# Two stacked transformer blocks: attention heads of the second block issued between its projections, and four difference heads per transpose

## What is computed

```python
proj = h @ w_in                      # 1024 x 2212
# c_q 384, c_kv 256, k_rope 32, dq dk dv 256 each, fq fk fv 256 each, ff 4
o_mla = mla_attention(rms_norm(c_q) @ w_uq, rms_norm(c_kv) @ w_ukv, k_rope)   # 8 heads, q and k 96 wide
o_diff = diff_attention(dq, dk, dv)  # 4 heads; each two softmaxes over q, k 32 wide
o_fox = forgetting_attention(fq, fk, fv, cumsum(log_sigmoid(ff + bias)))      # 4 heads, 64 wide
h = layer_norm(ALPHA * h + concat(o_mla, o_diff, o_fox) @ w_out)
h = layer_norm(ALPHA * h + grouped_moe(h))   # 16 experts, 2 chosen per token
```

## Time and profile before

| | us |
|---|---|
| median of 3 runs | 1852.04 (1848.75 to 1855.86) |
| profiled execution | 1850.06, its span 1848.3 |
| TensorE busy | 1588.5 (86%), granted clock 0.932 of full |
| VectorE busy | 938.5 (51%) |
| ScalarE busy | 622.3 (34%) |
| DMA | 231 GB/s over the span |
| layer 0: input projection's end to output projection's end | 990.7 to 1107.2 |
| layer 1: the same | 1442.0 to 1561.5 |

### The profile page before, as it was taken

How to read it: one execution, slowest core, us unless ns; L and a number is a source line. 1 busy time by engine, 2 the same in 40 slices (tenths; PEclk the granted TensorE clock), 3 DMA queues, 4 the chain that set the end, 5 groups by cost and what they waited for, 6 DMA issues and landing times.

```text
span 1848.3 us, 18868 instructions
## 1 busy us (share of the span) xinstructions
PE 1588.5 (86%) x7511; PEld 1095.8 (59%) x7511; DVE 938.5 (51%) x1346; ACT 622.3 (34%) x879; POOL 31.5 (2%) x62
## 2 busy tenths in 40 slices
PE   2889987999699987999977875999879696799985
PEld 2677766788587765888856763333327675433331
DVE  5896666855588665654375745111026575411002
ACT  1335534344334453444333631111124371211111
POOL 2000000000000000000030000000000000000000
PEclk9999998999899997999989886999999897799998
DMA  9676355856487433765464034999975404499994
GB/s 336 227 277 204 114 168 196 312 181 224 148 298 273 140 133 114 246 198 194 162 170 158 13 116 192 410 409 409 409 307 177 137 1 185 192 410 409 409 409 192
DMA packets 149964, 427.65 MB, mean 231 GB/s; under 512 B 8105, under 2 KB 16545, under 8 KB 149873
## 3 DMA queue, kind: packets, MB, share of 16 engines
q1 hardware_dynamic: 146192, 417.43, 61.7%
q0 software_dynamic: 3456, 8.87, 1.7%
q10 hardware_dynamic: 224, 0.07, 0.0%
HBM read 425.30 MB, written 1.05 MB: 231 GB/s over the span
## 4 chain that ended last, share of the span: by engine, by line
PE 45%; DVE 7%; SPq 6%; DMA 2%; ACT 1%; issue 1%; DVEq 0%
PE gp L1978 12%; PE gp L2150 9%; PE gp L2310 8%; SPq L702 6%; PE gp L2329 4%; PE mp L2350 2%; DMA raw_more<-in_exp_w_up 2%; PE gp L2295 2%; PE mp L2169 1%; PE mp L2208 1%; PE mp L2219 1%; PE mp L2218 1%; PE mp L2227 1%; DVE stats L1573 1%; DVE wlo L1153 0%
## 5 line engine op out<-in xcount | busy, mean ns | idle before, releaser
L1226 DVE TENSOR_TENSOR wlo<-raw,whi 128x2048 fp32r<-128x2048 f32 (+1 forms) x132 | 289.5, 2193 | 223.0 <-ACT whi L803 221.9
L803 ACT ACTIVATE whi<-raw 128x2048 fp32r<-128x2048 f32 (+1 forms) x132 | 242.2, 1836 | 365.3 <-PE gp L1978 200.5
L1978 PE MATMUL gp<-whi,xt_hi 128*128 128x512 f32 (+1 forms) x800 | 317.4, 397 | 32.2 <-DVE xt_lo L1275 14.1
L1978 PE MATMUL gp<-wlo,xt_hi 128*128 128x512 f32 (+1 forms) x800 | 311.3, 389 | 0.0
L1978 PE MATMUL gp<-whi,xt_lo 128*128 128x512 f32 (+1 forms) x800 | 311.1, 389 | 0.0
L1978 PEld LDWEIGHTS gp<-whi,xt_hi 128*128 128x128 f32 x800 | 154.6, 193 | 72.6 <-DVE wlo L1226 17.7
L1978 PEld LDWEIGHTS gp<-whi,xt_lo 128*128 128x128 f32 x800 | 154.3, 193 | 31.1
L1978 PEld LDWEIGHTS gp<-wlo,xt_hi 128*128 128x128 f32 x800 | 154.7, 193 | 29.1 <-issue 0.2
L1846 DVE TENSOR_SCALAR pr<-slots,key,dg 128x128 f32<-128x128 f32 x64 | 19.3, 344 | 260.1 <-PE gp L2340 260.1
L1153 DVE TENSOR_TENSOR wlo<-raw,whi 128x2048 fp32r<-128x2048 f32 (+3 forms) x36 | 68.3, 1906 | 42.4 <-ACT whi L949 41.8
L1136 DVE SCALAR_TENSOR_TENSOR acc<-raw,cact,acc 128x1024 f32<-128x1024 f32 x69 | 88.4, 1282 | 1.5
(11 more groups left out here) (384 smaller groups left out, 2352.1 us busy)
## 6 DMA issues: line engine op xcount, KB each, us to landing
raw<-in_w_in SPq DMA_DIRECT2D x60, 1024.0 KB, 6.0
raw<-in_w_ada SPq DMA_DIRECT2D x42, 1024.0 KB, 5.4
raw_deep<-in_exp_w_down SPq DMA_DIRECT2D x36, 1024.0 KB, 16.9
raw_deep<-in_exp_w_gate SPq DMA_DIRECT2D x30, 1024.0 KB, 14.4
raw_deep<-in_exp_w_up SPq DMA_DIRECT2D x30, 1024.0 KB, 16.8
raw<-in_w_gate SPq DMA_DIRECT2D x20, 1024.0 KB, 5.2
raw<-in_w_up SPq DMA_DIRECT2D x20, 1024.0 KB, 5.2
raw<-in_w_down SPq DMA_DIRECT2D x20, 1024.0 KB, 5.0
```

Source lines behind the costliest of these rows:

```text
L803: act.activation(slot(whi, s % SPLIT, units, cols), slot(raw, g % RAW, units, cols), ACT.Copy).then_inc(hi_done.sem, 1)
L1226: dve.tensor_tensor(slot(wlo, s % SPLIT, units, cols), slot(raw, g % RAW, units, cols), slot(whi, s % SPLIT, units, cols).bitcast(F32), AL ...
L1978: mm = pe.matmul(gp[:, q % 2, t, 0:wide], a[:, chunk, ts], w[:, unit, c0:c0 + wide], start=first and n == 0 and m == 0, stop=last and n == ...
```

## The change

- The column groups of the input projection are taken in reverse: the 164-column group (last part of fv, and the gates) first, c_q and c_kv last.
- Jobs are reordered: fox (4), diff (8), MLA (8). Each engine's part of step i becomes a function `attend(i)`. Steps 0 to 3 follow input products 6 to 9, steps 4 to 7 stand around the latents' norm and transposes, steps 8 to 11 follow the four up-projection products, and steps 12 to 23 run alone.
- Gates' logarithms, cumulative sum, fox operands, rotations of the diff heads and of the shared key are moved under the input products; the latents' norm moves behind the last of them. The latents are transposed into banks of `gp`, since `mp` is in use.
- Four halves of diff heads lie side by side in 128 columns, so q and k are transposed for four jobs at once (2 turns in place of 8); scores then read rows 0, 32, 64 or 96 of `qkt`.
- Token half 0 of keys and values is copied by ScalarE.
- The difference's first three stages are issued behind steps 16 to 18 on VectorE. Of the turned result, columns 0 to 511 (MLA heads) are transposed before the output projection, the others after its first product; the difference's last stage stands between.

The core of the diff (leading blanks cut):

```diff
+IN2_COLS = [(COLS * j, min(COLS, IN2 - COLS * j)) for j in reversed(range(IN2_JOBS))]
...
+JOBS = [MH + 2 * DH + i for i in range(FH)] + [MH + i for i in range(2 * DH)] + list(range(MH))
+FIRST_DIFF, FIRST_MLA = FH, FH + 2 * DH
+TOGETHER = P // DW
+TURNED = FH + 2 * DH // TOGETHER + MH
...
+def turn_of(i):
+    if i < FIRST_DIFF:
+        return i
+    return FIRST_DIFF + (i - FIRST_DIFF) // TOGETHER if i < FIRST_MLA else i - FIRST_MLA + TURNED - MH
+IN_STEPS = 4
+NORM_STEPS = IN_STEPS + 3
...
+def turned_here(i):
+    return i < AJ and (i == 0 or turn_of(i) != turn_of(i - 1))
+def turn_width(i):
+    return P if FIRST_DIFF <= i < FIRST_MLA else job_width(JOBS[i])
 def job_operands(j):
...
+latent_banks = (gp[:, 1, 0, :], gp[:, 1, 1, :], gp[:, 0, 0, :])
...
+    def attend(i):
+        if turned_here(i):
+            act.wait_ge(*t2_done.at2(l, turn_of(i) + 1))
+            w = turn_width(i)
+            act.activation(qkt[0:w, turn_of(i) % 2, :], mp[0:w, 0, :], ACT.Copy).then_inc(t2_taken.sem, 1)
...
+    high_x(X2_IN)
+    for s in range(S2_UQ):
+        split(s + 2)
+        if s % 2:
+            c, wide = IN2_COLS[s // 2]
...
+        if s >= S2_UQ - IN_STEPS:
+            attend(s - (S2_UQ - IN_STEPS))
+    act.wait_ge(*pair_free[0].at2(l, 6))
+    act.wait_ge(*pair_free[1].at2(l, 4))
+    for t in range(NT):
+        act.activation(rt1[:, 0:CQ], pr[:, t, 0:CQ], ACT.Square, accum_out=lsum4[:, t:t + 1]).then_inc(mla_sq.sem, 1)
+        act.activation(rt2[:, 0:CKV], pr[:, t, CQ:CQ + CKV], ACT.Square, accum_out=lsum4[:, 2 + t:3 + t]).then_inc(mla_sq.sem, 1)
+        act.wait_ge(*mla_sq.at2(l, 2 * t + 2))
+    attend(IN_STEPS)
+    act.wait_ge(*rv2_ready.at2(l, 1))
+    act.activation(rs[:, 0:4], rv[:, 0:4], ACT.Sqrt).then_inc(rs2_ready.sem, 1)
+    for i in range(IN_STEPS + 1, NORM_STEPS):
+        attend(i)
+    for b in range(3):
+        n = 2 if b < 2 else 1
+        high(latent_banks[b], X2_MLA + b, mt_hi[:, 2 * b:2 * b + n, :], n)
+    attend(NORM_STEPS)
+    for s in range(S2_UQ, S2_OUT):
+        split(s + 2)
+        q = J2_UQ + s - S2_UQ
+        h = 4 * ((s - S2_UQ) % 2)
+        if s < S2_UKV:
+            take(q, qm[:, 0, h:h + 4, :].rearrange("p h d -> p (h d)"))
+        else:
+            kv = gp[:, q % 2, 0, :].rearrange("p (h d) -> p h d", h=4)
+            act.wait_ge(*w_used.at2(l, job2_end(q) + 1))
+            act.activation(km[:, 0, h:h + 4, 0:MN], kv[:, :, 0:MN], ACT.Copy).then_inc(kv_taken.sem, 1)
+            act.activation(vm[:, 0, h:h + 4, :], kv[:, :, MN:MN + HD], ACT.Copy).then_inc(kv_taken.sem, 1)
+            act.wait_ge(*kv_taken.at2(l, 2 * (s - S2_UKV) + 2))
+            act.sem_inc(pair_free[q % 2].sem, 1)
+        attend(NORM_STEPS + 1 + s - S2_UQ)
...
+    def forget_gates(stage):
+        if stage == 0:
+            dve.wait_ge(*pair_free[0].at2(l, 2))
+            lk(dve.tensor_tensor(fz[:, :, :], pr[:, :, C_FF:C_FF + FH], fbc[:, :].unsqueeze(1).broadcast_to((P, NT, FH)), ALU.add))
+            lk(dve.tensor_scalar(fe[:, :, :], fz[:, :, :], -1.0, None, ALU.mult))
+            dve.tensor_tensor(fe[:, :, :], fz[:, :, :], fe[:, :, :], ALU.min).then_inc(fz_ready.sem, 1)
+        if stage == 1:
+            dve.wait_ge(*lam_exp.at2(l, 1))
+            lk(dve.tensor_tensor(nlam[:, :], lame[:, 1:2], lame[:, 0:1], ALU.subtract))
+            lk(dve.tensor_tensor(nlam[:, :], nlam[:, :], lami[:, :], ALU.subtract))
+            dve.wait_ge(*fl_ready.at2(l, 1))
+            lk(dve.tensor_scalar(fz[:, :, :], fz[:, :, :], 0.0, None, ALU.min))
+            dve.tensor_tensor(fz[:, :, :], fz[:, :, :], fl[:, :, :], ALU.subtract).then_inc(logf_ready.sem, 1)
+        if stage == 2:
+            dve.wait_ge(*pair_free[1].at2(l, 2))
+            dve.wait_ge(*pair_free[0].at2(l, 4))
+            up = HD ** 0.5
+            for dst, c in ((fq, C_FQ), (fk, C_FK)):
+                lk(dve.tensor_copy(dst[:, :, :, 0:HD], pr[:, :, c:c + FH * HD].rearrange("p t (h d) -> p t h d", d=HD)))
+            lk(dve.memset(fq[:, :, :, HD + 1:HD + 2], 1.0))
+            lk(dve.memset(fk[:, :, :, HD:HD + 1], 1.0))
+            dve.wait_ge(*cum_done.at2(l, 1))
+            cum = mp[:, 3, 0:NT * FH].rearrange("p (t h) -> p t h", t=NT)
+            lk(dve.tensor_scalar(fq[:, :, :, HD:HD + 1].rearrange("p t h a -> p t (h a)"), cum, up, None, ALU.mult))
+            dve.tensor_scalar(fk[:, :, :, HD + 1:HD + 2].rearrange("p t h a -> p t (h a)"), cum, -up, None, ALU.mult).then_inc(fox_ready.sem, 1)
+    def rotate_diff():
+        dve.wait_ge(*pair_free[1].at2(l, 4))
+        for c in (C_DQ, C_DK):
+            rotate(pr[:, :, c:c + 2 * DH * DW].rearrange("p t (h d) -> p t h d", d=DW)[:, :, :, 0:DROT], 2, 2 * DH, DROT)
+        dve.sem_inc(diff_ready.sem, 1)
+    def shared_key():
+        kr = pr[:, :, C_KR:C_KR + KR].unsqueeze(2)
+        rotate(kr, 1, 1, KR)
+        lk(dve.tensor_copy(km[:, :, :, MN:MQ], kr.broadcast_to((P, NT, MH, KR))))
     d1 = oa[:, :, HD * MH:HD * (MH + DH)]
-    lk(dve.scalar_tensor_tensor(out=d1, in0=od[:, :, :], scalar=nlam[:, :], in1=d1, op0=ALU.mult, op1=ALU.add))
-    lk(dve.tensor_tensor(od[:, :, :], d1, d1, ALU.mult))
-    n = NT * DH
-    lk(dve.tensor_reduce(rt[:, 0:n].rearrange("p (t h) -> p t h", t=NT), od[:, :, :].rearrange("p t (h d) -> p t h d", d=HD), AX.X, ALU.add))
-    dve.tensor_scalar(rv[:, 0:n], rt[:, 0:n], 1.0 / HD, EPS, ALU.mult, ALU.add).then_inc(rv2_ready.sem, 1)
-    reciprocal_root(n, rs2_ready.at2(l, 2), lk)
     d1h = d1.rearrange("p t (h d) -> p t h d", d=HD)
-    lk(dve.tensor_tensor(d1h, d1h, rr[:, 0:n].rearrange("p (t h) -> p t h", t=NT).unsqueeze(3).broadcast_to((P, NT, DH, HD)), ALU.mult))
-    dve.tensor_tensor(d1h, d1h, subc[:, :].unsqueeze(1).unsqueeze(1).broadcast_to((P, NT, DH, HD)), ALU.mult).then_inc(oa_ready.sem, 1)
-    spread(X2_O, (2, 2, 2, 2), (xt_hi, xt_lo))
+    pairs = NT * DH
+    def difference(stage):
+        if stage == 0:
+            dve.wait_ge(*o2_taken.at2(l, FIRST_MLA))
+            lk(dve.scalar_tensor_tensor(out=d1, in0=od[:, :, :], scalar=nlam[:, :], in1=d1, op0=ALU.mult, op1=ALU.add))
+        if stage == 1:
+            lk(dve.tensor_tensor(od[:, :, :], d1, d1, ALU.mult))
+        if stage == 2:
+            lk(dve.tensor_reduce(rt[:, 0:pairs].rearrange("p (t h) -> p t h", t=NT), od[:, :, :].rearrange("p t (h d) -> p t h d", d=HD), AX.X, ALU.add))
+            dve.tensor_scalar(rv[:, 0:pairs], rt[:, 0:pairs], 1.0 / HD, EPS, ALU.mult, ALU.add).then_inc(rv2_ready.sem, 1)
+        if stage == 3:
+            reciprocal_root(pairs, rs2_ready.at2(l, 2), lk)
+            lk(dve.tensor_tensor(d1h, d1h, rr[:, 0:pairs].rearrange("p (t h) -> p t h", t=NT).unsqueeze(3).broadcast_to((P, NT, DH, HD)), ALU.mult))
+            dve.tensor_tensor(d1h, d1h, subc[:, :].unsqueeze(1).unsqueeze(1).broadcast_to((P, NT, DH, HD)), ALU.mult).then_inc(oa_ready.sem, 1)
+    turned_banks = [mp[:, b, :] for b in range(4)]
+    if l > 0:
+        split2(0, l)
+    spread(X2_IN, (2, 2, 2, 2), (xt_hi, xt_lo), turned_banks)
+    split2(1, l)
+    for s in range(S2_UQ):
+        split2(s + 2, l)
+        if s % 2:
+            c, wide = IN2_COLS[s // 2]
+            take(s // 2, 1, pr[:, 1, c:c + wide])
+        if s == 1:
+            small_parameters()
+            forget_gates(0)
+        if s == 2:
+            forget_gates(1)
+        if s == 5:
+            forget_gates(2)
+        if s == 7:
+            rotate_diff()
+        if s >= S2_UQ - IN_STEPS:
+            attend(s - (S2_UQ - IN_STEPS))
+        if s == 8:
+            shared_key()
+    dve.wait_ge(*mla_sq.at2(l, 4))
+    lk(dve.tensor_scalar(rv[:, 0:2], lsum4[:, 0:2], 1.0 / CQ, EPS, ALU.mult, ALU.add))
+    dve.tensor_scalar(rv[:, 2:4], lsum4[:, 2:4], 1.0 / CKV, EPS, ALU.mult, ALU.add).then_inc(rv2_ready.sem, 1)
+    attend(IN_STEPS)
+    reciprocal_root(4, rs2_ready.at2(l, 1), lk)
+    for t in range(NT):
+        for i, (a, b) in enumerate(((0, CQ), (CQ, CQ + CKV))):
+            lk(dve.scalar_tensor_tensor(out=pr[:, t, a:b], in0=pr[:, t, a:b], scalar=rr[:, 2 * i + t:2 * i + t + 1],
+                                        in1=cgc[:, a:b], op0=ALU.mult, op1=ALU.mult))
+    dve.sem_inc(mla_ready.sem, 1)
+    for i in range(IN_STEPS + 1, NORM_STEPS):
+        attend(i)
+    spread(X2_MLA, (2, 2, 1), (mt_hi, mt_lo), latent_banks)
+    attend(NORM_STEPS)
+    for s in range(S2_UQ, S2_OUT):
+        split2(s + 2, l)
+        q = J2_UQ + s - S2_UQ
+        h = 4 * ((s - S2_UQ) % 2)
+        if s < S2_UKV:
+            take(q, 1, qm[:, 1, h:h + 4, :].rearrange("p h d -> p (h d)"))
+        else:
+            kv = gp[:, q % 2, 1, :].rearrange("p (h d) -> p h d", h=4)
+            dve.wait_ge(*w_used.at2(l, job2_end(q) + 1))
+            lk(dve.tensor_copy(km[:, 1, h:h + 4, 0:MN], kv[:, :, 0:MN]))
+            dve.tensor_copy(vm[:, 1, h:h + 4, :], kv[:, :, MN:MN + HD]).then_inc(pair_free[q % 2].sem, 1)
+        attend(NORM_STEPS + 1 + s - S2_UQ)
+        if s == S2_UKV - 1:
```

(58 more changed lines are left out.)

204 lines of the change are left out of this document (45 added, 159 removed).

## The result

| | before | changed |
|---|---|---|
| median of 13 runs each | 1856.03 us (1847.67 to 1860.28) | 1843.16 us (1839.15 to 1850.26) |
| ratio, 95% interval | | 0.994 [0.9924, 0.9956] |
| profiled execution | 1850.06, span 1848.3 | 1843.52, span 1841.7 |

The change makes the kernel 0.6% faster, 12.9 us by the medians; 26 were forecast. The forecast started from a median of 1852.04 for the kernel before, from three runs; over these 13 it is 4.0 us higher. In the two profiled executions the second block's first transposes start at 937.48 before and at 943.51 after. The first block is not changed, and over the profiles of all kernels here this start lies anywhere from 937.5 to 947.9, so I compare each layer from its own start.

The account below looks back on a forecast made before the run. TensorE was taken as the bound between the head pipeline's fill and drain. Terms from input projection's end to output projection's end summed to 103.4 us against 116.5, gaining 13.1 a layer, 26 for both: 1826 us, range 1808 to 1843.

Parts of the forecast that it names:

- Steps 0 to 2 and the sum: Input projection: TensorE's part of the first three head steps, 3.1 us, with the moved cumulative sum 3.8 us a layer.
- The norm's stretch: From last input product to queries' product, with five steps: 20.8 us, including a 4.4 us wait for VectorE's maxima.
- Up-projections: Four up-projection products with steps 8 to 11: 23.0 us, including a 3.0 us TensorE wait; before, 21.8 with no steps.
- The table load without a drain: Norm's stretch: a ScalarE table load costs about 1.3 us; the page's added 1.38 us drain was not counted.
- For a restart at the lower clock ... I take 1.0: Steps 12 onward: restarting at the lower clock after 3 us of waiting costs 1.0 us, bounds nothing and 3.5.
- Four products 21.8: Output projection at each layer's end: its four products take 21.8 us.
- I make it nothing ... without cover it is up to 2.3 us once: Input projection, narrow units first: splits of following units covered by a long product, cost nothing; uncovered, up to 2.3 us once.
- Diff turns: Head steps of difference heads: two turns in place of eight, six times 0.45, 2.7 us less a layer.
- Scores on rows 32 to 96: Difference heads' scores on other array rows: taken as 0.85 us; could be 0.4 less or 0.85 more.
- The difference's stages and the output in halves: Layer's end: stages add 1.2 us; 2.7 from last scaling to first product; second product waits 2.5; before, 5.2 plus 3.4.
- less comes through: Waits at the norm and ahead of step 12 cost 3 us more each, difference stages 1; time 1840; chance 0.14.
- Rival 4: From step 5 to last weighing the clock stays low through heads and products: 16 us a layer lost, about 1884; chance 0.07.

Follow-up runs that it names:

- n1: Changed kernel with VectorE doing step 5 (scores and maxima) before the latents' root and scalings instead of after: 1834.73 us, ratio 0.9895 to before.
- t1: Changed kernel with useless filling transposes behind steps 20 to 23 and ahead of the first and second output products: 1832.72 us, ratio 0.9883 to before.
- g3: Changed kernel with the gates' work spread over units 2, 3 and 4 and TensorE's sum behind product 5: 1837.60 us, ratio 0.9906 to before.
- d1: Changed kernel with each diff half turned by itself again, eight turns of 32 columns instead of two: 1841.26 us, ratio 0.9936 to before.
- p1: Kernel before with only the new end: difference's first three stages behind the last steps, output turned in halves: 1854.33 us, ratio 0.9987.
- s1: Changed kernel with all 24 head steps alone behind the last up-projection product, none between products or around the norm: 1890.48 us, ratio 1.0183 to before.
- s5: s1 with eight diff turns of 32 columns, heads in the changed order (fox, difference, MLA): 1892.72 us, ratio 1.0195 to before.
- s4: s3 with each difference half turned by itself again, eight turns, scores on rows 0 to 31: 1863.07 us, ratio 1.0052 to before.
- s3: s1 with the jobs in the order of the kernel before (MLA, diff, fox): 1889.47 us, ratio 1.0170 to before.
- m1: Changed kernel with the edits of g3, n1 and t1 together, plus 18 more filling transposes ahead of step 12: 1813.76 us, ratio 0.9781 to before.
- b1: Kernel before with useless transposes: 34 ahead of the cumulative sum, 66 ahead of the heads, 48 ahead of the output's transposes: 1850.37 us, ratio 0.9973.
- s2: s1 with 70 useless filling transposes ahead of the first head step: 1893.53 us, ratio 1.0205 to before.

## Why the prediction was wrong

1826 was forecast, with a gain of 26 us; the gain was 12.9 and the time 1843.16, a hair past the upper end of the range. The sign was right and the size a factor of two off. Against the table of layers, the miss is 6.3 and 5.1 us at the end of the two layers and 4.2 in layer 1's input projection; in layer 1 the norm's stretch and the up-projections add 2.9, and layer 0's input projection was 1.2 below. By its own steps:

- **Steps 0 to 2 and the sum, 3.8 us: right and a little high.** Layer 0's projection grew by 2.6 us. TensorE's own part was the whole price there.
- **The norm's stretch, 20.8 us: right in layer 0**, 21.0, and 1.8 over in layer 1; the wait on VectorE's maxima was 4.62 against 4.4 forecast. n1 shows that this wait was a matter of order, worth 3 to 4 us a layer. I had found it, priced it and not asked whether it need be.
- **Up-projections, 23.0 us: right in layer 0**, 23.1, and 1.1 over in layer 1; the wait ahead of step 12 was 2.63 against 3.0.
- **The table load without a drain: right.** Two table loads follow one another in the norm's stretch, and each is followed by its activation. In ScalarE's timeline above the load of 1006.32 took 1.28 and the root began at 1007.61; the next load followed at 1007.84 and the exponential at 1009.13. The Trainium skill's page ScalarE: Activation LUTs, section What ACT_TABLE_LOAD costs, has a drain of 1.38 us beside each load; this trace has none.
- **"For a restart at the lower clock ... I take 1.0", and nothing for the end: this is the step that failed.** The restart cost 2.5 us in layer 0 (two steps of 7.1 us for 4.6) and as much in layer 1, so it was 1.5 short. What I left at the full level was everything behind: the drain in layer 0, and in both layers the first output transposes and the first output product. Against the table above, the last three stretches are 6.3 us over forecast in layer 0 and 5.1 in layer 1. "Four products 21.8" is four times the long product's 5.44, all at the full level; the first one measured 8.00 and 8.64. Even in the kernel before the four took 22.7 (1084.50 to 1107.2), since the first began cold, though with 16 transposes right ahead of it (1081.1 to 1084.8). TensorE's timeline of the kernel before, just behind its matmul of 1084.50:

```profile
1085.09 0.63 PE L2150 MATMUL gp<-wlo,xt_hi 128*128 128x512 f32 x1
1085.52 0.52 PE L2150 MATMUL gp<-whi,xt_lo 128*128 128x512 f32 x1
1085.88 0.40 PE L2150 MATMUL gp<-whi,xt_hi 128*128 128x512 f32 x1
```

Three of its 24 matmuls were slow, and one in layer 1. In the changed kernel 8 transposes stand there with a pause behind them, and 11 of 24 were slow in layer 0, 14 in layer 1. t1 filled the pauses and got 10 us back, so this cause is shown. Halving the work ahead of the product, which the change did to start it sooner, also made it start cold.
- **The input projection, "I make it nothing ... without cover it is up to 2.3 us once": failed in layer 1.** A stall of 2.84 us, and the product behind it 7.37 us for 5.44. I had looked at the splits and not at the gates between them. The gates go from VectorE to ScalarE, back to VectorE and on to TensorE, and the change put them behind the second unit, where the narrow units leave the least cover. g3 moved them apart and got 5 us back; shown.
- **Diff turns, 2.7 us a layer: nothing** (d1). TensorE was given 0.45 us less in steps where, after the change, it was waiting for VectorE anyway. My own count had VectorE behind in both new stretches, and that should have told me so. Scores on rows 32 to 96 cost 0.85 as I had taken.
- **The difference's stages and the output in halves: about nothing** by p1, though the pause of 5.2 us a layer is gone from it. The wait ahead of the second product, which the sum had, and the cold first product, which it had not, took it back.

The nearest rival was the first, "less comes through", with 1840: it blamed the lower clock, but in the wrong places. It set 3 us at the norm's wait and 3 ahead of step 12, and the loss was at the end. Rival 4, the clock low through heads and products, did not come; s1 shows that its price was real (46 us in all, where 29 a layer were priced) in the arrangement without products between the heads. What the interleaving itself is worth depends on what it is measured against. s5 and d1 differ in the place of the steps alone and lie 48 us apart. Much of that is the low clock: from the last up-projection product to the output's transposes s5 takes 77.7 us, s4, whose clock stays up, 60.7. s4, with the MLA heads first, keeps its clock up and is 10 us slower than before, where the changed kernel is 12 faster. By that measure some 20 us came from putting steps between products, and some 10 were lost by what else s4 has from the change, the new order of columns and the open norm above all. That is a subtraction over kernels that also differ in the order of the heads; no run takes it apart.

What stays open: why the clock falls in s3 and not in s4 (the transposes, the rows of the scores or ScalarE's copies), and why it then rises in s3's fox heads and not in s1's. Which part of m1's filling gives how much was not taken apart.

## What to carry to other kernels

When work is moved off a stretch so that the next product can start sooner, look at the clock at which that product will start: a pause removed in front of it can come back inside it. Sum a step's engines in the order of their queues, and where a wait of some microseconds comes out, try the other order of the two pieces on the engine that is late before you accept the wait. A hand-over between two engines that both also split weights belongs one unit apart at each crossing.

## What the hardware did that I had not expected

- A run of nothing but fp32 128x128 transposes raised the granted clock from 0.50 to 1.00 within 7.3 us (b1), and useless ones in the pauses of the end (8, 4, 4, 6 and 9 ahead of the first output product, 9 ahead of the second) held it at 1.00, which was worth 10 us (t1).
- A TensorE that is busy without a gap can stay at the lower level: 26.0 of 26 us at 0.50 in s1, in steps of fox and difference heads, and 20.0 of 20 in s3 with difference heads. The first MLA heads brought it up in s1, s2 and s5, fox heads in s3.
- Whether difference heads are turned each by itself or four at once (0.45 us of transposes a step, other rows for the scores) decided in s4 and s3 between 1.00 and 0.50, and 22 us of the whole.
